# Two feature tiles of a 31-tap convolution: ScalarE products and GpSimd additions in place of diagonal matrices on TensorE

## The reference, cut to what matters

```python
CONV_WIDTH_2 = 31
def _conformer_conv(a, gate, conv_w, conv_b, ln_g, ln_b, w_out):
    u = a * jax.nn.sigmoid(gate)
    u = lax.conv_general_dilated(
        u, conv_w[:, None, :].astype(u.dtype), window_strides=(1,),
        padding=[(CONV_WIDTH_2 - 1, 0)], dimension_numbers=('NWC', 'WIO', 'NWC'),
        feature_group_count=CONV_CH) + conv_b
    u = jax.nn.silu(_layernorm(u, ln_g, ln_b))
    return u @ w_out
...
y_conv = _conformer_conv(c_a, c_g, conv_w[l], conv_b[l], conv_ln_g[l], conv_ln_b[l], w_conv_out[l])
y_attn = _dsa_attention(qh, kh, vh, qih, kih, wih) @ w_attn_out[l]
h = h + (g_conv * y_conv + g_attn * y_attn) @ w_mix_out[l]
```

## Time and profile before

| what | value |
|---|---|
| three runs | 1073.03, 1071.45, 1068.76 us; median 1071.45 |
| the profiled execution | 1072.58 us, its span 1070.7 us |
| PE busy | 1000.0 us, 93% of the span |
| DVE busy | 711.5 us, 66% |
| ACT busy | 553.1 us, 52% |
| POOL busy | 12.6 us, 1%, in 20 instructions |
| mean granted TensorE clock | 0.971 |

### The profile page before, as it was taken

How to read it: one execution, slowest core, us unless ns; L and a number is a source line. 1 busy time by engine, 2 the same in 40 slices (tenths; PEclk the granted TensorE clock), 3 DMA queues, 4 the chain that set the end, 5 groups by cost and what they waited for, 6 DMA issues and landing times.

```text
span 1070.7 us, 13652 instructions
## 1 busy us (share of the span) xinstructions
PE 1000.0 (93%) x5045; PEld 826.5 (77%) x5045; DVE 711.5 (66%) x1254; ACT 553.1 (52%) x986; POOL 12.6 (1%) x20
## 2 busy tenths in 40 slices
PE   4988999998799999999999989999999889999996
PEld 4777766775687888888888778888887768888885
DVE  4545667543676666665787999886577667666564
ACT  5532465655355455444653445665484565544542
POOL 0000000000000000000000000000000000000000
PEclk8988999998899999999998989999999999999999
DMA  8644234443544665665554435444446524566551
GB/s 289 192 119 119 62 115 120 136 138 108 168 157 158 196 191 164 206 198 189 179 154 119 126 111 157 128 129 148 148 143 211 150 86 158 180 210 200 183 171 40
DMA packets 86961, 164.78 MB, mean 154 GB/s; under 512 B 8176, under 2 KB 9328, under 8 KB 86768
## 3 DMA queue, kind: packets, MB, share of 16 engines
q1 hardware_dynamic: 86896, 163.91, 49.3%
HBM read 162.84 MB, written 1.05 MB: 153 GB/s over the span
## 4 chain that ended last, share of the span: by engine, by line
PE 80%; DVE 12%; ACT 3%; DMA 2%; issue 2%; POOL 1%; SPq 0%; DVEq 0%; ACTq 0%
PE pb L355 77%; DVE wlo L1090 3%; PE pb L359 3%; DVE YC L1384 2%; ACT whi L724 1%; DMA raw<-in_w_in 1%; POOL ST L1574 1%; DVE SC L1357 1%; DMA WC<-in_wcmp 1%; DMA MEM<-in_mem 1%; DVE ST L1353 0%; DVE U L1106 0%; DVE HF L1106 0%; DVE CC L1262 0%; DVE ST L1546 0%
## 5 line engine op out<-in xcount | busy, mean ns | idle before, releaser
L1090 DVE TENSOR_TENSOR wlo<-raw,whi 128x1024 fp32r<-128x1024 f32 (+1 forms) x302 | 362.5, 1213 | 257.0 <-ACT whi L724 256.0
L724 ACT ACTIVATE whi<-raw 128x1024 fp32r<-128x1024 f32 (+1 forms) x302 | 311.9, 1046 | 235.5 <-PE pb L355 231.4
L355 PE MATMUL pb<-XT,whi 128*128 128x512 f32 x1032 | 382.2, 411 | 20.7 <-DVE wlo L1090 10.0
L355 PE MATMUL pb<-XT,wlo 128*128 128x256 f32 x1032 | 293.7, 285 | 0.0
L355 PEld LDWEIGHTS pb<-XT,whi 128*128 128x128 f32 x1032 | 198.7, 192 | 77.8 <-DVE wlo L1090 13.5
L355 PE MATMUL pb<-whi,ZT 128*128 128x512 f32 x640 | 203.5, 394 | 0.0
L355 PEld LDWEIGHTS pb<-XT,wlo 128*128 128x128 f32 x1032 | 199.6, 193 | 0.8
L355 PE MATMUL pb<-whi,XT 128*128 128x512 f32 (+2 forms) x576 | 187.2, 394 | 5.7 <-DVE XT L1135 3.7
L355 PEld LDWEIGHTS pb<-whi,ZT 128*128 128x128 f32 x640 | 121.2, 189 | 26.9 <-issue 0.9
L355 PEld LDWEIGHTS pb<-whi,XT 128*128 128x128 f32 x576 | 108.6, 192 | 28.2 <-DVE wlo L1090 3.9
L355 PE MATMUL pb<-wlo,ZT 128*128 128x512 f32 x320 | 125.5, 392 | 0.0
(11 more groups left out here) (186 smaller groups left out, 790.9 us busy)
## 6 DMA issues: line engine op xcount, KB each, us to landing
raw<-in_w_in SPq DMA_DIRECT2D x108, 512.0 KB, 3.6
raw<-in_w_ff SPq DMA_DIRECT2D x64, 512.0 KB, 4.3
raw<-in_w_up SPq DMA_DIRECT2D x32, 512.0 KB, 4.5
raw<-in_w_down SPq DMA_DIRECT2D x32, 512.0 KB, 4.2
raw<-in_w_branch_b SPq DMA_DIRECT2D x8, 512.0 KB, 3.7
raw<-in_w_out SPq DMA_DIRECT2D x8, 512.0 KB, 3.8
raw<-in_wx_kv SPq DMA_DIRECT2D x8, 512.0 KB, 4.0
raw<-in_w_attn_out SPq DMA_DIRECT2D x8, 512.0 KB, 3.4
```

Of the source, the lines that this page charges most:

```text
L355: return e.matmul(o, l, r, start=start, stop=stop, skip_group_check=True)
L724: return e.activation(o, i, ACT.Copy, scale=scale)
L1090: e.tensor_tensor(wlo[u % NW][:, 0:c], raw[u % NRAW][:, 0:c], whi[u % NW][:, 0:c].bitcast(F32), ALU.subtract).then_inc(lo, 1)
```

## The change

Tiles 6 and 7 of the convolution leave TensorE. ScalarE now multiplies the shifted 128x256 piece of `U2` by the tap's weights: for tap 0 straight into `YC` with the bias, for the 30 others into one of three buffers `TP`. GpSimd adds each `TP` to `YC` in place (60 additions, tiles 6 and 7 in turn). The products start two steps earlier than the diagonals did (8 skipped calls in place of 10), two a step. The diagonals, the 62 matmuls of `conv_taps` and the two `conv_out` copies are gone. `TP` lies where `GA2` will be, so VectorE waits for the 60th addition before it writes `GA2`.

```diff
 GAIN = {T_X: "norm1", T_MEM: "normmem", T_2: "norm2", T_MIX: "normmix", T_XA: "normx", T_FFN: "normffn"}
-PE_CONV = 6
+DVE_CONV = 6
...
-        DG = sb("DG", 4 * P)
...
+        TP = work(W0 + 14064, "TP", 768)
...
-        dg_made, cv_done, y_made, cv_out = sem("diagonal_made"), sem("conv_tap_done"), sem("y_made"), sem("conv_copied")
+        tap_made, y_added, y_made = sem("tap_product"), sem("tap_added"), sem("y_made")
...
-            def conv_taps():
-                for _ in range(10):
-                    yield
-                for f in range(PE_CONV, 8):
-                    e.wait_ge(u2_made, f + 1)
-                    for k in range(31):
-                        n = 31 * (f - PE_CONV) + k
-                        e.wait_ge(dg_made, n + 1)
-                        mm(PB[f][:, 0:256], DG[:, P * (n % 4):P * (n % 4) + P], U2[:, f, k:k + 256], k == 0,
-                           k == 30).then_inc(cv_done, 1)
-                        if n % 2:
-                            yield
...
-                        e.wait_ge(*(o_lo, 4 + h) if h else (cv_out, 1))
+                        if h:
+                            e.wait_ge(o_lo, 4 + h)
...
-                e.wait_ge(y_made, PE_CONV)
-                e.wait_ge(cv_out, 8 - PE_CONV)
+                e.wait_ge(y_made, DVE_CONV)
+                e.wait_ge(y_added, 60)
...
-            side, taps = attention2(), conv_taps()
+            side = attention2()
             for name in ("b2_cg1", "b2_ca1", "b2_k0", "b2_k1", "b2_q0", "b2_q1"):
-                cols(name, XT, ready, side, taps)
+                cols(name, XT, ready, side)
...
-            def diagonals():
-                for _ in range(10):
+            def tap_products():
+                for _ in range(8):
                     yield
-                for n in range(31 * (8 - PE_CONV)):
-                    if n >= 4:
-                        e.wait_ge(cv_done, n - 3)
-                    copy(DG[:, P * (n % 4):P * (n % 4) + P], ident,
-                         prm("convw2", 8 * (n % 31) + PE_CONV + n // 31)).then_inc(dg_made, 1)
+                for n in range(62):
+                    k, f = n // 2, DVE_CONV + n % 2
+                    if n < 2:
+                        e.wait_ge(u2_made, f + 1)
+                        e.activation(YC[:, f, :], U2[:, f, 0:256], ACT.Identity, scale=prm("convw2", f),
+                                     bias=prm("convb2", f)).then_inc(tap_made, 1)
+                    else:
+                        if n >= 5:
+                            e.wait_ge(y_added, n - 4)
+                        copy(TP[:, 256 * (n % 3):256 * (n % 3) + 256], U2[:, f, k:k + 256],
+                             prm("convw2", 8 * k + f)).then_inc(tap_made, 1)
                     if n % 2:
                         yield
...
-            side, diag = attention2(), diagonals()
+            side, prod = attention2(), tap_products()
             for name in ("b2_cg1", "b2_ca1", "b2_k0", "b2_k1", "b2_q0", "b2_q1"):
-                run(name, side, diag)
+                run(name, side, prod)
...
-                    if s == 27:
-                        conv_out(6)
...
-            def conv_out(f):
-                e.wait_ge(cv_done, 31 * (f - PE_CONV) + 31)
-                e.tensor_scalar(YC[:, f, :], PB[f][:, 0:256], prm("convb2", f), None, ALU.add).then_inc(cv_out, 1)
...
+                e.wait_ge(y_added, 60)
...
                 run(name, side, taps)
+                if k == 2:
+                    e.wait_ge(y_added, 60)
                 gate_out(k, name, G, k % 2)
             now(taps)
-            conv_out(7)
             norm = conv_norm()
...
-            for n in range(N_MEM, N_END + 1):
+            for n in range(N_MEM, N_MIX + 1):
+                norm(n)
+            for n in range(2, 62):
+                f = DVE_CONV + n % 2
+                e.wait_ge(tap_made, n + 1)
+                if n >= 4:
+                    e.wait_ge(y_added, n - 3)
+                e.tensor_tensor(YC[:, f, :], YC[:, f, :], TP[:, 256 * (n % 3):256 * (n % 3) + 256],
+                                ALU.add).then_inc(y_added, 1)
+            for n in range(N_XA, N_END + 1):
```

More of the change, by code:

```diff
@@ L669, in tensor_program @@
             i.then_inc(unit_done, 1)
-            side, taps = attention2(), conv_taps()
+            side = attention2()
             for name in ("b2_cg1", "b2_ca1", "b2_k0", "b2_k1", "b2_q0", "b2_q1"):
-                cols(name, XT, ready, side, taps)
+                cols(name, XT, ready, side)
             for name in ("b2_v0", "b2_v1", "b2_gc0", "b2_gc1"):
-                rows(name, XT, ready, side, taps)
+                rows(name, XT, ready, side)
             norm = conv_norm()
-            rows("b2_ga0", XT, ready, side, taps)
-            now(taps)
+            rows("b2_ga0", XT, ready, side)
             rows("b2_ga1", XT, ready, side, norm)
@@ L1027, in scalar_program @@
                         copy_out(name, t, V2[:, t, 512 * i:512 * i + 512])
-            run("b2_ga0", side, diag)
-            now(diag)
+            run("b2_ga0", side, prod)
+            now(prod)
             norm = conv_norm()
@@ L1374, in taps2 @@
                 n, made = 0, {}
-                for f0 in range(0, PE_CONV, 2):
+                for f0 in range(0, DVE_CONV, 2):
                     for k in range(31):
```

## The result

The changed kernel took 1081.7 us (median of 10 runs), the kernel before on the same chip 1070.93 us. The ratio is 1.0096, 95% interval 1.0075 to 1.0116: slower by about 10 us. The profiled execution took 1083.75 us, its span is 1082.0 us.

What follows compares the result with a forecast made beforehand. VectorE was taken to bound steps 8 to 19 and, slowed by GpSimd's reads, steps 20 to 39 instead of TensorE. 9.0 + 4.8 - 4.0 - 0.7 = +9.1 us gave a forecast of 1081 us, range 1059 to 1104.

Steps and rivals of the forecast that it cites:

- Who bounds what: 602.62 to 738.87 us: VectorE sets the pace in the first 51.07 us, and the new length of the rest too.
- A: Steps 8 to 19, 602.62 to 653.69 us: VectorE-bound, TensorE's saving worth nothing; forecast +9.0 us.
- the hold: VectorE's taps and wlo, reading two SBUF tiles, lose 0.43 us per GpSimd addition, 60 additions; forecast's chance 45%.
- B: Steps 20 to 39, 653.69 to 738.87 us: TensorE busy throughout before; VectorE then needs 89.9 against 85.2 us, +4.8.
- pairs: Two tap matmuls on TensorE (four records), 0.68 us together; 31 go, 21.1 us of TensorE in all.
- the sum: Steps 8 on: 9.0 + 4.8 - 4.0 - 0.7 = +9.1 us, making the profiled execution 1081.7 us.
- fast rival: GpSimd's reads hold nothing; steps 20 to 39 shrink by 7.6 to 11.6 us, about 1062 us; chance 27%.
- given back: After step 39: a late VectorE lets TensorE run up to two units further, 4.0 us regained (0 to 6.7).
- the stretch: The part the change touches, from VectorE's step 8 to the layer norm; forecast +9.1 us.
- What I said would show it: From step 8: VectorE's taps and wlo 26 us longer together, chain on VectorE till about 750 us, TensorE gaps from step 20.
- second rival: Each addition holds VectorE for its whole 0.98 us: +42 us, about 1113, or 1099 at 75% meeting; chance 12%.
- step 8: VectorE's step at 602.62 us in the kernel before, where the forecast's VectorE-bound first part begins.

Runs made afterwards that it cites:

- run without products: Changed kernel without taps 1 to 30 of tiles 6 and 7: no ScalarE products, no GpSimd additions, only tap 0; 1057.71 us, ratio 0.9855 to the kernel before.
- one-column run: Changed kernel, but each of the 60 GpSimd additions covers 1 of 256 columns, all products and waits kept; 1058.49 us, ratio 0.9859 to the kernel before.
- PSUM sums: Changed kernel with all its work, but VectorE keeps its taps' running sums in PSUM bank 7; 1058.92 us, ratio 0.9871 to the kernel before.
- one tile: Changed kernel, but tile 6 stays on TensorE and only tile 7 goes to ScalarE and GpSimd; 1063.14 us, ratio 0.9916 to the kernel before.
- additions on the kernel before: Kernel before, its tap matmuls kept on TensorE, plus 60 GpSimd additions of 128x256 on scratch; 1078.77 us, ratio 1.0049.

## Why the prediction was right

Forecast 1081, measured 1081.7; the way to it, point by point:

- **Who bounds what.** VectorE in A, and with the hold VectorE in B too: right. Without a hold A stays as it was (51.07 to 51.37 us in three runs) though TensorE has lost 10 pairs there. But "VectorE, not TensorE, sets B's new length" is right only with the hold. In the run without products the chain goes back to TensorE at 665.46 us and stays there. Two units of that chain, before and without products:

```profile
704.81 8.56 PE pb L355 x40
713.70 8.53 PE pb L355 x40
...
696.10 6.85 PE pb L355 x32
703.28 6.83 PE pb L355 x32
```

The eight records that are gone are two pairs. From start to start two units take 8.89 us before and 7.18 without them. So a pair is worth 0.86 us there, not the 0.68 of the sum, and TensorE's saving in B was put too low: 20 pairs are 17.1 us, not 13.6. From step 20 to the layer norm that run needs 87.7 us for 103.4 before, 15.7 less, and TensorE is busy for 85.8 of them. This did not touch the forecast, in which VectorE sets the pace. But the fast rival, "nothing held", took B as VectorE's 73.6 us and nothing as given back behind it, 8 to 12 us in all with the last pair where 15.7 came; so it was put at 1062, and the runs without a hold came out at 1058.
- **The hold** was the step on which all hung. 0.43 us an addition was taken from VectorE's own time for 256 columns; measured, VectorE's busy time is 23.3 us above the one-column run (733.2 against 709.9), 0.39 each. The size came out near by two errors that offset each other: a held instruction loses mostly 0.48 us, more than 0.43, but only 50 of VectorE's instructions were held, by more than 0.06 us, beside the 60 additions (39 taps, seven wlo, two first taps, two score instructions, 23.1 us in all), where the sum let every addition hold one. That step was argued from no direct row; three kinds of runs have now shown the hold (fewer columns, writes alone, inputs from PSUM).
- **Stage A** +7.2 for +9.0, **stage B** +4.9 for +4.8. In A TensorE waits for VectorE in three places, 21.9 us, as said, and its clock is lower (0.86 for 0.93). That costs nothing: the run without products has a clock of 0.87 in A and the same length of A as before, 51.07 us.
- **Given back at the end**: 5.6 for 4.7 with the last pair.
- **The total** came nearer than its parts. The sum said +9.1 us for the stretch; the two pairs of traces have +6.5 and +5.7. That 1081 met 1081.7 is in part luck, since some 4 us of the measured 10 lie outside the stretch.
- **ScalarE** pays 0.45 us a product (27.1/60) for 0.34 a diagonal and hides it: the two runs with and without products take the same time. **GpSimd** takes 0.94 us for 0.98.
- **What I said would show it**: longer taps and wlo came, 17.6 and 3.7 us in the page's sums; the chain stays with VectorE to 748 us but for one piece; B has gaps on TensorE.

The lock for the whole instruction (Trainium skill, SBUF — State Buffer, "Who interferes with whom") was the second rival. Its part on who is held is borne out for VectorE's instructions with two SBUF tiles as input; the length is not. An undisturbed addition takes 0.73 us and holds a tap for 0.55 at most; an instruction of one column takes 0.19 us undisturbed (0.33 in the median) and holds nothing that shows. By 60 holds of 0.98 us the time would have been about 1113.

Not settled: the stretch and the 1.4 us by which step 8 comes later in both traces of the changed kernel make 7 to 8 us of the 10.3 by the ratio (interval 8 to 12). Step 8 comes ahead of the first addition in every kernel of the table, anywhere from 600.3 to 604.0, so I don't put the 1.4 down to the change. In the later pair on one chip, one run of each kernel, the difference was 4.9 us, with 5.7 in the stretch. In the runs of one column, no products, PSUM sums and one tile the ratio and the stretch agree within 1 us (1.5 for the additions on the kernel before); of the changed kernel's 10.3 us some 4 are left without a cause. Why the clock falls in the cross attention in some executions was not tried.

## What to carry to other kernels

An engine that looks free is not free when its reads hold another one: before moving element-wise work to GpSimd, ask what VectorE is doing there, and how much of it reads two SBUF tiles. Where the bound is an average, find the stretch: TensorE, busy 93% of the span, had a stage of 51 us in which its time was worth nothing. If the work is to move anyway, keep VectorE's running sum in PSUM where a bank is free; that turned +10 us into -14 here, each against its own runs of the kernel before.

## What the runs showed of the hardware that was not expected

- VectorE's scalar_tensor_tensor with its running sum in PSUM takes 484 ns for 128x256, as long as with both tiles in SBUF (477 ns), and no GpSimd addition holds it. GpSimd gains as well: 0.74 us an addition in the median in place of 0.92.
- The hold is shorter than the instruction that causes it and goes with what that reads: at most 0.55 us for 256 columns added (instruction 0.73), 0.27 for 128 (0.45), 0.20 for 256 copied (0.40), none for 256 written (0.31). Each of the three is the undisturbed instruction less some 0.19 us, and 0.19 us is what one of one column takes undisturbed. That would fit a hold for the reading part alone; no run tested it further.
- A tensor_scalar with one SBUF tile as input and SBUF as output can be held too: in the changed kernel the two of six that met an addition took 823 and 829 ns in place of 406. Written to PSUM, all six took 535 to 547 ns, the two beside an addition 535 and 540. So two SBUF tiles as input are not the only case, and why this one is held was not tried.
